# A decoder layer with 64 experts: the second product of long steps on two and four column groups

## The reference

```python
def swiglu(x, w1, w3, w2):
    return (jax.nn.silu(x @ w1) * (x @ w3)) @ w2
...
    def run_block(args):
        e, toks, g = args
        xb = xpad[toks]
        hb = jax.nn.silu(xb @ w1_e[e]) * (xb @ w3_e[e])
        return (hb @ w2_e[e]) * g[:, None].astype(xb.dtype)
...
    y = swiglu(xf, w1_s, w3_s, w2_s) + routed_experts(xf, idx, gates, w1_e, w3_e, w2_e)
```

## Time and profile before

| what | value |
|---|---|
| runs | 1188.8, 1189.84, 1190.72 us; median 1189.84 |
| profiled execution | 1188.33 us, span 1186.6 us from first to last instruction |
| granted TensorE clock over the span, mean | 0.987 |
| TensorE matmuls busy | 1129.1 us (95% of the span) |
| VectorE, ScalarE, GpSimd busy | 427.9, 256.9, 254.0 us |
| DMA | 319.16 MB, mean 269 GB/s over the span |

### The profile page before, as it was taken

How to read it: one execution, slowest core, us unless ns; L and a number is a source line. 1 busy time by engine, 2 the same in 40 slices (tenths; PEclk the granted TensorE clock), 3 DMA queues, 4 the chain that set the end, 5 groups by cost and what they waited for, 6 DMA issues and landing times.

```text
span 1186.6 us, 21423 instructions
## 1 busy us (share of the span) xinstructions
PE 1129.1 (95%) x8348; PEld 752.3 (63%) x8348; DVE 427.9 (36%) x1127; ACT 256.9 (22%) x533; POOL 254.0 (21%) x292
## 2 busy tenths in 40 slices
PE   7999996999999988989999999999999999999996
PEld 6888654877875767857765555555555565555521
DVE  0359998233039434661112222122222222221034
ACT  1101144013042124201122222222222222222210
POOL 3120050000000000032333333433323333333300
PEclk9999998999998999999999999999999999999999
DMA  9630304015045652185999999999999999999696
GB/s 331 250 142 1 152 21 177 1 75 227 1 143 176 250 214 108 73 286 197 365 408 392 396 383 394 402 399 388 383 386 402 393 384 384 381 401 387 260 369 279
DMA packets 67593, 319.16 MB, mean 269 GB/s; under 512 B 11591, under 2 KB 17951, under 8 KB 40909
## 3 DMA queue, kind: packets, MB, share of 16 engines
q1 hardware_dynamic: 51269, 278.60, 60.3%
q0 software_dynamic: 14848, 35.48, 7.9%
q10 hardware_dynamic: 1424, 4.35, 0.9%
HBM read 300.15 MB, written 29.36 MB: 278 GB/s over the span
## 4 chain that ended last, share of the span: by engine, by line
PE 74%; DVE 16%; DMA 4%; ACT 2%; SPq 2%; issue 1%; POOL 0%; DVEq 0%; POOLq 0%
PE psum L797 66%; PE psum L812 8%; DVE act_mem L1782 7%; DVE mk_mem L1944 2%; DMA arena<-y_rows 2%; DMA arena<-in_w_in_dram 1%; SPq L572 1%; DMA act_mem<-x_rows,more_x 1%; DVE act_mem L2000 0%; ACT act_mem L1565 0%; DVE act_mem L2151 0%; DVE act_mem L1879 0%; ACT act_mem L1574 0%; DVE act_mem L1796 0%; DVE act_mem L2163 0%
## 5 line engine op out<-in xcount | busy, mean ns | idle before, releaser
L797 PE MATMUL psum<-arena,act_mem 128*32 128x128 f32 (+6 forms) x4800 | 507.8, 361 | 0.9 <-ACT act_mem L1665 0.9
L797 PEld LDWEIGHTS psum<-arena,act_mem 128*32 128x32 f32 (+5 forms) x4800 | 259.7, 123 | 188.8 <-issue 107.9
L797 PE MATMUL psum<-act_mem,arena 128*128 128x260 f32 (+1 forms) x1728 | 355.1, 367 | 8.2 <-DMA arena<-in_w_in_dram 2.8
L797 PEld LDWEIGHTS psum<-act_mem,arena 128*128 128x128 f32 x1728 | 307.9, 194 | 52.8 <-DMA arena<-in_w_in_dram 3.0
L705 POOL DMA_INDIRECT y_rows<-act_mem,idx_y x39 | 45.9, 1177 | 239.3 <-DVE act_mem L2201 226.3
L812 PE MATMUL psum<-ident,act_mem 128*128 128x128 f32 (+6 forms) x484 | 80.0, 297 | 17.2 <-DVE act_mem L1883 6.8
L2201 DVE TENSOR_SCALAR act_mem<-psum,act_mem 96x512 f32<-96x512 f32 (+1 forms) x40 | 29.9, 747 | 159.7 <-PE psum L797 159.7
L1782 DVE SCALAR_TENSOR_TENSOR act_mem<-act_mem,wcb 128x511 f32<-128x511 f32 (+29 forms) x120 | 77.8, 729 | 0.0
L812 PEld LDWEIGHTS psum<-ident,act_mem 128*128 128x128 f32 (+6 forms) x484 | 58.5, 172 | 29.6 <-issue 13.7
L2198 DVE TENSOR_TENSOR act_mem<-act_mem,psum 128x192 f32<-128x192 f32 x35 | 12.4, 355 | 161.2 <-ACT act_mem L1636 161.2
L797 PEld LDWEIGHTS psum<-act_mem 128*96 128x96 bf16 (+7 forms) x419 | 31.3, 125 | 60.7 <-issue 59.7
(11 more groups left out here) (282 smaller groups left out, 789.6 us busy)
## 6 DMA issues: line engine op xcount, KB each, us to landing
arena<-in_w_e_dram SPq DMA_DIRECT2D x192, 1024.0 KB, 9.8
arena<-y_rows SPq DMA_DIRECT2D x8, 2048.0 KB, 24.2
arena<-in_w_in_dram SPq DMA_DIRECT2D x16, 512.0 KB, 18.0
arena<-in_cache_mem_k_dram SPq DMA_DIRECT2D x8, 1024.0 KB, 8.6
arena<-in_cache_mem_v_dram SPq DMA_DIRECT2D x8, 1024.0 KB, 12.1
arena<-in_w_v_dram SPq DMA_DIRECT2D x1, 4096.0 KB, 24.7
arena<-in_w_k_dram SPq DMA_DIRECT2D x1, 4096.0 KB, 14.0
arena<-in_w_out_dram SPq DMA_DIRECT2D x1, 4096.0 KB, 14.0
```

Source lines behind the costliest of these rows:

```text
L797: return pe.matmul(out, lhsT, rhs, start=first, stop=last)
```

## The change

The second product of long steps is put on column groups like the first: `down_most` multiplies the first 64 slots in two halves of the outputs (partitions 0 to 63 of the bank hold outputs 0 to 511, 64 to 127 hold 512 to 1023) and the other 32 slots in four quarters. A result slot then lies on several partitions, so the gate can't be a per-partition scale of the result as simply as before. It is applied to the hidden values instead, which lie on the same layout: `spread_gates` copies each gate to the partitions where `hd_most` needs it. Emptying the bank becomes three copies on each engine (`yh_most`, in the diff first that of ScalarE, then that of VectorE). The big steps and the light ones stay as they are.

```diff
+            def down_most(b, part):
+                _, wd = ew(part)
+                for k in range(2):
+                    for h in range(2):
+                        mm(psum[LCAP * h:LCAP * h + LCAP, 0, 0:512], hidT[:, b, MCAP * k:MCAP * k + LCAP],
+                           wd[:, k, 512 * h:512 * h + 512], k == 0, k == 1)
+                for k in range(2):
+                    for q in range(4):
+                        last = mm(psum[MORE * q:MORE * q + MORE, 0, 512:768], hidT[:, b, MCAP * k + LCAP:MCAP * k + MCAP],
+                                  wd[:, k, 256 * q:256 * q + 256], k == 0, k == 1)
+                return last
...
-                    down(n % 2, n % 4, CAP if is_big(e) else MCAP).then_inc(m_y, 1)
+                    (down if is_big(e) else down_most)(n % 2, n % 4).then_inc(m_y, 1)
...
+            def yh_most(out):
+                act.activation(out[0:LCAP, 0:512], psum[0:LCAP, 0, 0:512], ACT.Copy)
+                for q in range(2):
+                    last = act.activation(out[LCAP:MCAP, 256 * q:256 * q + 256],
+                                          psum[MORE * q:MORE * q + MORE, 0, 512:768], ACT.Copy)
+                return last
...
-            def indices(n, s, base_count, cap=CAP, split=True):
+            def indices(n, s, base_count, cap=CAP, split=True, spread=False):
...
+                if spread:
+                    spread_gates(n)
                 return dve.tensor_scalar(idx_x[0:cap, n:n + 1], idx_y[0:cap, n:n + 1], 3, None, ALU.logical_shift_right)
...
-            def hd_most(b):
-                return dve.tensor_tensor(silu[:, b, 0:192], silu[:, b, 0:192], psum[:, 2, 512 * b + 192:512 * b + 384], ALU.mult)
+            def hd_most(b, n):
+                dve.scalar_tensor_tensor(silu[:, b, 0:P], silu[:, b, 0:P], gates[:, n, 0:1],
+                                         psum[:, 2, 512 * b + 192:512 * b + 320], ALU.mult, ALU.mult)
+                return dve.scalar_tensor_tensor(silu[:, b, P:192], silu[:, b, P:192], gates[:, n, 1:2],
+                                                psum[:, 2, 512 * b + 320:512 * b + 384], ALU.mult, ALU.mult)
+            def yh_most(out):
+                dve.tensor_copy(out[0:LCAP, 512:1024], psum[LCAP:2 * LCAP, 0, 0:512])
+                for q in range(2, 4):
+                    last = dve.tensor_copy(out[LCAP:MCAP, 256 * q:256 * q + 256], psum[MORE * q:MORE * q + MORE, 0, 512:768])
+                return last
+            def spread_gates(n):
+                for h in range(2):
+                    dve.tensor_copy(gates[LCAP * h:LCAP * h + LCAP, n, 0:1], picked[0:LCAP, n, 1:2])
+                for q in range(4):
+                    dve.tensor_copy(gates[MORE * q:MORE * q + MORE, n, 1:2], picked[LCAP:MCAP, n, 1:2])
...
+                    dve.wait_ge(m_idx, e + 1)
+                    hd_most(n % 2, n).then_inc(m_hd, 1)
```

More of the change, by code:

```diff
@@ L243, in decoder_step @@
         swT = act_mem[:, A4 + 1296:A4 + 1296 + T]
+        gates = act_mem[:, A4 + 1860:A4 + 1860 + 2 * NB].rearrange("p (n c) -> p n c", c=2)
         idx_y = sb("idx_y", [P, NB], U32)
@@ L1684, in y_step @@
                     yh_few(n % 2, n).then_inc(m_ya, 1)
+                elif is_big(e):
+                    yh(ys[:, n % 2, :], n).then_inc(m_ya, 1)
                 else:
-                    yh(ys[:, n % 2, :], n, CAP if is_big(e) else MCAP).then_inc(m_ya, 1)
+                    yh_most(ys[:, n % 2, :]).then_inc(m_ya, 1)
             def step(e, k, i, sc):
@@ L2221, in i_step @@
                 else:
-                    indices(n, m_iv, 2 * e, CAP if is_big(e) else MCAP).then_inc(m_idx, 1)
+                    indices(n, m_iv, 2 * e, CAP if is_big(e) else MCAP, spread=not is_big(e)).then_inc(m_idx, 1)
             def c_step(e, n):
@@ L2227, in c_step @@
                     dve.wait_ge(m_y, e - 1)
-                (hd_few if is_light(n) else hd if is_big(e) else hd_most)(n % 2).then_inc(m_hd, 1)
+                if is_light(n) or is_big(e):
+                    (hd_few if is_light(n) else hd)(n % 2).then_inc(m_hd, 1)
+                else:
+                    dve.wait_ge(m_idx, e + 1)
+                    hd_most(n % 2, n).then_inc(m_hd, 1)
             def y_step(e, k, i, sc):
@@ L2237, in y_step @@
                     dve.wait_ge(m_sm[n % 2], 16 * halves_out(i, k - 2, 2))
-                yh(ys[:, n % 2, :], n, CAP if is_big(e) else MCAP).then_inc(m_yv, 1)
+                (yh(ys[:, n % 2, :], n) if is_big(e) else yh_most(ys[:, n % 2, :])).then_inc(m_yv, 1)
             oh_step(0, 0)
```

## The result

The changed kernel takes 1206.22 us (median; 1202.87 to 1207.0) against 1190.2 us for the kernel before: ratio 1.0134, 95% interval 1.0116 to 1.0152, so 16 us slower where 15 us faster was forecast. The profiled execution has a span of 1204.3 us.

What follows compares the result with a forecast made beforehand. TensorE was taken to bound the kernel, with DMA nearly full. Saving 20.7 us less 5.6 us of gather waits gave 15.1 us, so 1175 us from the 1189.84 median; range 1166 to 1184, likeliest case 1169 to 1181.

Steps and rivals of the forecast that it cites:

- The 16 additional weight loads of a step are of 32 columns and lie beside the matmuls: TensorE, second product of long steps: the added weight loads were taken to cost no extra time.
- TensorE's step becomes 9.44 - 0.59 x 5/8 = 9.07: Expert loop on TensorE: average step falls from 9.44 to 9.07 us, or 9.17 with gather waits.
- A to E: Forecast cases: the sum, 0.60; DMA holds the pace, 0.19; whole saving arrives, 0.11; slow emptying, 0.07; groups not together, 0.03.
- Second product: TensorE, long steps: 2.85 us against 3.44, saving 0.59 a step, 20.7 us (16 to 25) over 35 steps.
- rival E: TensorE, 32-slot part: four groups don't run together at 256 outputs; 14 us lost, 1204 us; chance 0.03.
- the sum: Whole kernel: 20.7 us saved on TensorE less 5.6 us of gather waits, a gain of 15.1 us.
- The 0.26 us: TensorE, 32-slot part: assumed fixed cost of a change of grouping, unpaid at bound 0.85 us, paid whole at 1.11.
- Rival C: Whole saving arrives: gathers land early and grouping is cheap; gain 21 to 25 us, 1165 to 1168; chance 0.11.
- Emptying the bank and the gates: ScalarE copies 1.35 us, VectorE 1.61, done about 0.86 us later; gate copies at most 0.85 us, hidden by scatters.
- rival D: Emptying the bank becomes the loop's clock, making 14 edge gathers late; 1197 us at 2 us each; chance 0.07.
- Gathers: Gathered rows at two places in eight arrive late: 0.4 us each, 14 places, 5.6 us (0 to 20).
- the forecast's worst price for DMA: DMA work per step, by share, 9.25 us: 4.5 us over 56 steps, within the weights' 6.2 us to spare.

Runs made afterwards that it cites:

- the loop written out: The changed kernel with TensorE's hardware loop over eights written out, other engines keeping their loops: 1179.55 us, ratio 0.9922 to the kernel before.

## Why the prediction was wrong, step by step

**What failed** is this step: "The 16 additional weight loads of a step are of 32 columns and lie beside the matmuls", and with it "TensorE's step becomes 9.44 - 0.59 x 5/8 = 9.07". Their execution does lie beside the matmuls. But weight loads and matmuls were priced by their time alone, and the 32 instructions that a step gained were never counted against the hardware loop that holds them. No rival named that either; A to E all take the instructions to be there when their turn comes. The trace of before had evidence of what could be lost: 37 blocks of instructions for the whole run, and none between 684 and 1068 us, so the body was being kept. How much longer it could become was not to be read from it. What the runs showed in place of a free set of instructions is five stalls of 3.67 to 3.97 us, one for each jump back, and a longer product behind each.

**The price.** From expert 8 to expert 61 the changed kernel takes 1123.81 - 605.83 = 517.98 us against 500.27, 17.7 us more. Five stalls are 19.2, the products behind them 8.0, more waits for gathers 4.2 - 1.2 = 3.0; the 33 long second products in the stretch give back 33 x 0.45 = 14.9. That sums to 15.3 and leaves 2.4 us. The transposes between stall and product take 0.7 of them (0.56 to 0.69 us instead of 0.42 in three of the five turns); 1.7 us stay unplaced.

**Second product: right.** 2.88 us where 2.85 was forecast; four groups do run together (rival E out).

**Its entry: mis-sized.** From the start of the row transposes to the start of the second product it was 0.98 us ahead of `down` and is now 650.23 - 649.14 = 1.09. The light steps had paid that 0.11 all along, and the sum took only the product's own starts. The net saving is 3.44 - 2.88 - 0.11 = 0.45 a step, not 0.59, 35 x 0.45 = 16 us, at the low bound of the forecast's 16 to 25. The 0.26 us that those bounds gave a change of grouping stood in no row, and no run here shows it; what the runs show is this 0.11. Rival C was out of reach.

**Emptying the bank and the gates: right.** The groups by line and shape of after (busy us, mean ns of one):

```profile
L1670 ACT ACTIVATE act_mem<-psum 32x256 f32<-32x256 f32 x62 | 23.1, 373 | 0.7
L1668 ACT ACTIVATE act_mem<-psum 64x512 f32<-64x512 f32 x31 | 18.3, 591 | 71.0 <-PE psum L798 71.0
...
L2234 DVE COPY act_mem<-psum 32x256 f32<-32x256 f32 x62 | 26.4, 425 | 0.8
L2232 DVE COPY act_mem<-psum 64x512 f32<-64x512 f32 x31 | 21.5, 693 | 108.9 <-PE psum L798 108.9
L2242 DVE COPY act_mem<-act_mem 32x1 f32<-32x1 f32 x128 | 18.5, 145 | 1.7
```

591 + 2 x 373 ns = 1.34 us on ScalarE (forecast 1.35) and 693 + 2 x 425 = 1.54 on VectorE (1.61); a gate's copy is 145 ns (142). Emptying the bank in three copies was measured to change nothing by itself (ratio 1.0005). "TensorEngine Tiling (Array Packing)", PSUM Bottleneck, in the Trainium skill, cited for rival D, warns that this copy may become the bottleneck; here it didn't.

**Gathers: right in kind and size.** 4.2 us of waits in the changed kernel and 5.2 in the loop written out, against 1.2 before; 5.6 more was forecast, 4.0 more came with the loop written out. All six of its waits lie ahead of experts at positions 0 and 4, the two that were named. Part of them stand under "issue" in the view of waits: they lie ahead of the transposes of the gathered rows (`x8`), where TensorE waits for gathers, and are counted here by that place.

**DMA: no wait for weights, as forecast.** With the loop written out the share is 1.00 at 400 GB/s, a step takes (1097.72 - 607.33) / 53 = 9.25 us, and no wait for weights shows. That is just the forecast's worst price for DMA, 9.25, so whether DMA would have let this loop get any shorter stays open. The Trainium skill's 358 GB/s of HBM per core ("DMA: Bandwidth & Descriptors", Specifications) is passed here again.

Without the jumps the sum holds: 16 us of saving less 5.2 - 1.2 = 4.0 of additional gather waits would be 12, and the loop written out is 1189.48 - 1179.55 = 9.9 us faster than before.

## What to carry to other kernels

Count instructions as well as their time when work inside a hardware loop is cut into more pieces: read the instruction queue's row over the loop's turns first. It was empty there in the kernel before, whose loop was kept; a longer body no longer was. Here a loop that didn't fit showed as an idle time with no releaser at the first instruction of each turn, with blocks of program loaded around it. With the loop written out, the price was gone; with three turns instead of six, two stalls of five were left. Once the jumps were gone, the change was worth 10 us.

## What the runs showed of the hardware

- TensorE kept a loop body of about 1652 recorded instructions (one block loaded in 384 us) and didn't keep one of about 1684 (43 blocks). "Advanced Engine Details and Errata" of the Trainium skill, ISA Cache, gives 128 KB on TensorE in lines of 16 KB, 256 instructions each. The trace agrees on the 16 KB and on the 256: with the loop written out, 35 blocks go with 8994 recorded instructions of TensorE from 684 to 1068 us, 257 a block. By the page's figures an estimate of 2048 instructions would fit, and that is not what the runs show. Turns of the loop load more than they use: 44 blocks in 384 us where the loop written out loads 35 for more work, so loading seems to run past the jump, which may account for the difference. Where the body lies against the blocks may matter too; neither was tried.
- A jump back to program that is not kept cost a stall of 3.6 to 5.2 us, no longer for a body of sixteen steps (3.90 and 3.92) than for one of eight, and TensorE went on 1.5 to 1.7 us after the second block had landed. Straight code of the same instructions, whose blocks are loaded as well, had no such stall.
- Behind the first stall of the changed kernel the granted clock read 0.57 (694 to 698 us), and the first product behind each stall of all these kernels was 1.1 to 2.6 us longer than 5.82. An idle time of 1.53 us, ahead of the transposes at 676.51, left the products behind it at 2.94 and 5.82 us.
